# Scan stage: sample gate and old states in column tiles, new states in 32-row tiles, decay on GpSimd, clip per head

## The chip, the cores and the metric

The kernel runs on one core of one Trainium2 chip. The metric is device time in microseconds (us), the median of the runs. Five engines run side by side and wait for each other through semaphores: TensorE (PE; its weight loads are listed as PEld), VectorE (DVE), ScalarE (ACT), GpSimd (POOL) and SyncE (SP), which here only issues DMAs.

## What is computed

One step of a hybrid decoder layer for a prompt of 512 tokens and eight sample sequences of eight tokens: a combined input projection, latent attention, a Mamba-2 scan (SSD), a mixture of experts and two norms, all in float32. The change is in the scan. From the reference, cut:

```python
a_cs = jnp.cumsum(dt * a, axis=2)
seg = a_cs[:, :, :, None] - a_cs[:, :, None, :]
decay_ls = jnp.exp(jnp.where(causal[:, :, None, None], seg, -jnp.inf))
cb = jnp.einsum('bclgn,bcsgn->bclsg', cm, bm)
w_ls = cb[..., None] * decay_ls * dt[:, :, None]
y_diag = jnp.einsum('bclsgh,bcsghp->bclghp', w_ls, x)
states = jnp.einsum('bclgn,bclgh,bclghp->bcghpn', bm, decay_end * dt, x)
...
    return d_c[..., None, None] * h + s_c, h
...
y_off = jnp.einsum('bclgn,bcghpn->bclghp', cm, h_prev) * jnp.exp(a_cs)[..., None]
...
y = y.reshape(b, t, D_INNER) * jax.nn.silu(z.astype(jnp.float32))
y = rms_norm(y.reshape(b, t, SSD_GROUPS, D_INNER // SSD_GROUPS), ...)
```

There are four groups of eight heads (`G`, `HG`), a head has 64 channels (`PD`), a state 128 entries (`NST`). The prompt goes in four chunks of 128 tokens. A sample sequence is one chunk of eight tokens with an old state from `state_ssm`, and its new state is an output.

## The kernel before

The program is a chain of stages, each with one instruction stream per engine and a barrier of all engines behind it. `stage_ssd` holds the scan. It runs over N = 20 units k = (g, i): four groups g of five tiles i, the tiles 0 to 3 being prompt chunks of 128 tokens (called P0 to P3 in the prediction) and tile 4 the 64 sample tokens (called S). In a group the prompt tiles pass a state `stT` along; tile 4 works with the old states `h0` of the eight sequences (four blocks of 128 channels, eight sequences, 128 entries).

The order on every engine is that of the code, written as a software pipeline over k. TensorE does per iteration: `inputs(k)` (four transposes of x into bank 0, L1426; B turned and C·B in bank 1, L1432 and L1433; for tile 4 the decays at the sequences' ends, L1439), `gate(k-1)` (eight products with the weights `wz` into bank 7, L1452), `turn(k-2)` (four transposes of the normed y, L1521) and `outputs(k-1)` (eight heads, L1464, into bank 4; state times C, L1467, into bank 5; the chunk's own state, L1470, into bank 6). A float32 product shows as two records in the trace.

For tile 4 `outputs` goes on: the final prompt state is turned (L1475) and copied by ScalarE to `st_out` (L1585); then for each of the eight sequences four transposes of its old state (L1489, alternately into banks 7 and 6), a copy to `h0T` on ScalarE (L1591) and a product with `c_of` (L1498), where C is masked to the sequence's tokens, summed in bank 5 of all 64 rows. Then eight products of `xend` and `b_of` (B masked by sequence, 64 rows), L1507, alternately into banks 6 and 7, each followed by an addition to `h0` on VectorE (L1703). The gate of the next group's tile 0 stands behind all eight (`hs_out`).

VectorE does per iteration k: copies of B and C·B (L1652, L1653), the clip of the decay exponents `dec` (subtract, L1663; minimum with 0, L1665), then, when ScalarE has taken the exponential (L1559), the product with C·B (L1668). Then for unit k-1: for tile 4 the aging of the old states, `h0` times `e_seq` (L1677), the output (from L1679 to the gate's product, L1690), the states (L1694, L1696, or L1703 for tile 4) and the norm (L1708, L1710, L1713). ScalarE: copy of x (L1557), exponential of `dec` (L1559), SiLU of the gate (L1567), copy of the turned y to `yT` (L1574, shown as xbcT), the copies above, square and root (L1595, L1597). The three functions each load a table. GpSimd scales x in three ways (L1390) and masks C and B (L1395, L1398). SP issues the decays of unit k+3 once unit k's output is ready, for tile 4 then the stores of `st_out` and, behind `hs_out`, of `h0`, and behind their landing the loads of the next group's old states.

## Time and profile before

| | us |
|---|---|
| median of 3 runs (2594.32 to 2598.78) | 2597.01 |
| the profiled execution's own time | 2604.68 |
| its span, first to last instruction | 2602.9 |
| its mean granted TensorE clock (share of 2.4 GHz) | 0.946 |
| TensorE busy in the span | 2404.9 (92%) |
| VectorE busy | 1838.8 (71%) |
| ScalarE busy | 1325.8 (51%) |
| GpSimd busy | 463.4 (18%) |

The scan stage lies between about 724 and 1117 us of the span. The time at which an engine is busy over the whole span says little about it; it has to be read from its own stretch. In a timeline a row gives the start, the length, the engine with the line and operation, what is written and read, and in brackets how long the engine was idle before and what released it. Rows of several instructions are merged (x16). Durations of matmuls overlap, since they are pipelined; the distance between starts is what one costs. In the rows by stretch the columns are: stretch, us, then busy time (and count) of PE, PEld, DVE, ACT and POOL, the granted clock, the share of the DMA engines, GB/s.

### The profile page before, as it was taken

Reading aid. Unit: us, or ns where it says so; the run is one execution under the profiler, and the core shown is the slowest. Engines: PE = TensorE matmul, PEld = TensorE weight load, DVE = VectorE, ACT = ScalarE, POOL = GpSimd, SP = SyncE. Lnnn points to the kernel's source line nnn. Section 1 sums busy time; section 2 is a strip of 40 time slices with the busy share of each in tenths; the row PEclk is TensorE's granted clock in tenths of the full one; section 3 lists DMA queues with packets and bytes.
Section 4 is the critical chain, followed back from the end, with each engine's and each line's share of the span. In section 5 each row is a group of like instructions: output and inputs, shape, how many; then the busy total and the mean of one; then the engine's idle time right before and its main releaser. Section 6 shows DMA issues by size and latency. Waiting matters only on the chain. (4 is left out here: it accounts for less than half of the span.)

```text
span 2602.9 us, 38413 instructions
## 1 busy us (share of the span) xinstructions
PE 2404.9 (92%) x14463; PEld 1889.6 (73%) x14463; DVE 1838.8 (71%) x2099; ACT 1325.8 (51%) x1410; POOL 463.4 (18%) x372
## 2 busy tenths in 40 slices
PE   8798999989969999979898999999999999999993
...
DMA packets 248575, 589.80 MB, mean 227 GB/s; under 512 B 28880, under 2 KB 120272, under 8 KB 243984
## 3 DMA queue, kind: packets, MB, share of 16 engines
...
## 5 line engine op out<-in xcount | busy, mean ns | idle before, releaser
L2418 DVE TENSOR_TENSOR w_lo<-w_raw,w_hi 128x2048 fp32r<-128x2048 f32 x291 | 660.2, 2289 | 56.1 <-ACT w_hi L2368 54.5
L2368 ACT ACTIVATE w_hi<-w_raw 128x2048 fp32r<-128x2048 f32 x288 | 550.2, 1916 | 130.4 <-PE banks L2311 118.7
L2311 PE MATMUL banks<-w_hi,x_hi 128*128 128x512 f32 x1024 | 319.9, 394 | 2.1 <-DVEq L2457 2.1
L2311 PE MATMUL banks<-w_lo,x_hi 128*128 128x512 f32 x1024 | 316.9, 391 | 0.0
L2311 PE MATMUL banks<-w_hi,x_lo 128*128 128x512 f32 x1024 | 316.3, 390 | 0.0
L2418 DVE TENSOR_TENSOR w_lo<-mergedT,w_hi 128x2048 fp32r<-128x2048 f32 x96 | 220.0, 2292 | 40.0 <-ACT w_hi L2368 39.8
L2311 PEld LDWEIGHTS banks<-w_hi,x_lo 128*128 128x128 f32 x1024 | 192.8, 188 | 41.0
L2311 PEld LDWEIGHTS banks<-w_lo,x_hi 128*128 128x128 f32 x1024 | 192.8, 188 | 40.9
L2311 PEld LDWEIGHTS banks<-w_hi,x_hi 128*128 128x128 f32 x1024 | 190.5, 189 | 40.0 <-DVEq L2457 2.1
L2271 POOL DMA_INDIRECT y_sum<-xT,to_row x32 | 50.9, 1590 | 845.6 <-ACT xT L2400 845.6
L2368 ACT ACTIVATE w_hi<-mergedT 128x2048 fp32r<-128x2048 f32 x96 | 183.8, 1915 | 34.0 <-PE banks L2311 30.5
L2311 PE MATMUL banks<-w_hi,h_hi 128*128 128x512 f32 x512 | 158.5, 391 | 0.0
L2311 PE MATMUL banks<-w_hi,h_lo 128*128 128x512 f32 x512 | 158.0, 390 | 0.0
L2311 PE MATMUL banks<-w_lo,h_hi 128*128 128x512 f32 x512 | 157.7, 389 | 0.0
L1452 PE MATMUL banks<-wz,xT 128*128 128x512 f32 (+1 forms) x320 | 147.8, 616 | 0.9 <-ACT zs L1567 0.9
L1452 PEld LDWEIGHTS banks<-wz,xT 128*128 128x128 f32 (+1 forms) x320 | 58.6, 188 | 76.3 <-issue 75.9
L2311 PEld LDWEIGHTS banks<-w_lo,h_hi 128*128 128x128 f32 x512 | 96.1, 188 | 20.8
L2311 PEld LDWEIGHTS banks<-w_hi,h_hi 128*128 128x128 f32 x512 | 96.0, 188 | 20.8 <-DVE w_lo L2418 0.3
L2311 PEld LDWEIGHTS banks<-w_hi,h_lo 128*128 128x128 f32 x512 | 96.1, 188 | 20.0
L1390 POOL TENSOR_TENSOR xdt<-xs_t,dt 128x512 f32<-128x512 f32 (+1 forms) x20 | 26.1, 1304 | 427.2 <-ACT xs_t L1557 427.2
L1034 PE MATMUL banks_a<-part_hi_a,w_mhi_a 128*128 128x288 f32 x384 | 83.2, 298 | 14.5 <-DVE w_mlo_a L1070 14.5
L1070 DVE TENSOR_TENSOR w_mlo_a<-w_raw_a,w_mhi_a 128x1024 fp32r<-128x1024 f32 x24 | 29.4, 1225 | 85.0 <-ACT w_mhi_a L1044 85.0
...
## 6 DMA issues: line engine op xcount, KB each, us to landing
...
```

Source lines behind the costliest of these rows:

```text
L1034: mm = pe.matmul(bank_of(u)[:, piece], wp[:, u % NW, k, :], part[:, piece * H2:(piece + 1) * H2], start=(k == 0 and wp is w_hi and n == 0) ...
L1070: dve.tensor_tensor(w_lo[:, u % NW], w_raw[:, u % NR], w_hi[:, u % NW].bitcast(F32), ALU.subtract).then_inc(w_low, 1)
L1390: ins = pool.tensor_tensor(heads(o[0:n, k % 2], n), x, f[:, g * HG:(g + 1) * HG].unsqueeze(2).broadcast_to((n, HG, PD)), ALU.mult)
L1452: mm = pe.matmul(banks[0:n, 7, :], sb.xT[:, q, P * i:P * i + n], wz[:, g % 2, q, :], start=(q == 0), stop=(q == KD - 1))
L2271: pool.indirect_dma_start(out=io.y_sum, out_offset=bass.IndirectOffsetOnAxis(ap=to_row[:, par, :].bitcast(U32), axis=0), in_=y_out, in_off ...
L2311: mm = pe.matmul(banks[:, bank + c, :], x[:, k, :], part[:, s % NHI, j, c * 512:(c + 1) * 512], start=start, stop=last)
L2368: act.activation(w_hi[:, s % NHI], raw(s, par), ACT.Copy).then_inc(hi_ready, 1)
L2418: dve.tensor_tensor(w_lo[:, s % NHI], raw(s, par), w_hi[:, s % NHI].bitcast(F32), ALU.subtract).then_inc(lo_ready, 1)
```

## The change

For the sample tile (i = 4):

- The gate is computed in two column tiles: 256 output columns each, with the 64 tokens on PSUM partitions 0 to 63 and 64 to 127 of bank 7, sixteen products of 256 columns for eight of 512. SiLU takes the two halves apart.
- Old states are turned in pairs j and j + 4 (eight transposes), into banks 2 and 3 or 6 and 7, copied to `h0T` (four places for two) by ScalarE and VectorE, one each, and multiplied with 32 columns of `c_of`, into partitions 0 to 31 and 32 to 63 of bank 5.
- New states: eight products of 32 rows in pairs (`new_part`, q = 0 to 3), the first pair at the end of `outputs`, the second behind the next `inputs`, the last two behind the next `gate`. The additions to `h0` go into `renew`, the first four ahead of the unit's norm, the last four behind it. The wait of the next gate for them is gone; a wait for the first six stands in `outputs` of the next group's tile 0.
- `h0` times `e_seq` goes to GpSimd, behind `b_of` and ahead of the next unit's scaling.

For every tile the clip is one instruction per head that subtracts the head's own sum and takes the minimum with 0, eight instructions for two. `c_of`, `e_seq` lie in the room of `t1` to `t3`, and a constant of four columns is added.

```diff
+        NEW_BANK = (2, 5, 5, 2)
...
-                        pool.tensor_tensor(c_of[:], sb.xbcT[:, 20 + g, SEQ:T].unsqueeze(1).broadcast_to((P, NSEQ, NS)),
-                                           K[:, K_BCOL:K_BCOL + NSEQ * NS].rearrange("p (b n) -> p b n", b=NSEQ), ALU.mult)
+                            pool.wait_ge(st_ready, NT * g)
+                        pool.tensor_tensor(c_of.rearrange("p (a b) x -> p a b x", a=2),
+                                           sb.xbcT[:, 20 + g, SEQ:T].rearrange("p (a x) -> p a x", a=2).unsqueeze(2).broadcast_to((P, 2, 4, 32)),
+                                           K[:, K_BCOL:K_BCOL + NSEQ * NS].rearrange("p (b n) -> p b n", b=NSEQ)[:, 0:4, 0:32].unsqueeze(1).broadcast_to((P, 2, 4, 32)),
+                                           ALU.mult)
                         pool.wait_ge(cb_out, k + 1)
-                        pool.tensor_tensor(b_of[:], b_t[0:NS, k % 2, :].unsqueeze(1).broadcast_to((NS, NSEQ, NST)),
-                                           K[0:NS, K_BROW:K_BROW + NSEQ].unsqueeze(2).broadcast_to((NS, NSEQ, NST)), ALU.mult).then_inc(of_seq, 1)
+                        pool.tensor_tensor(b_of[:], b_t[0:NS, k % 2, :].unsqueeze(1).broadcast_to((NS, 4, NST)),
+                                           K[0:NS, K_BMOD:K_BMOD + 4].unsqueeze(2).broadcast_to((NS, 4, NST)), ALU.mult).then_inc(of_seq, 1)
+                        pool.wait_ge(e_out, g + 1)
+                        for j in range(4):
+                            pool.wait_ge(hT_ready, 4 * g + j + 1)
+                            for b in (j, j + 4):
+                                ins = pool.tensor_tensor(h0[:, :, b, :], h0[:, :, b, :], e_seq[:, :, b:b + 1].broadcast_to((P, 4, NST)), ALU.mult)
+                            ins.then_inc(aged, 1)
...
-                    if g >= 1 and i == 0:
-                        pe.wait_ge(hs_out, 8 * g)
+                    if i == NT - 1:
+                        for q in range(KD):
+                            for c in range(2):
+                                mm = pe.matmul(banks[64 * c:64 * (c + 1), 7, 0:GW // 2], sb.xT[:, q, SEQ:T], wz[:, g % 2, q, c * (GW // 2):(c + 1) * (GW // 2)],
+                                               start=(q == 0), stop=(q == KD - 1))
+                        mm.then_inc(z_ready, 1)
+                        return
...
+                        if g >= 1 and i == 0:
+                            pe.wait_ge(hs_out, 8 * g - 2)
                         pe.matmul(banks[0:n, 5, :], sb.xbcT[:, 20 + g, at], stT[:], start=True, stop=True).then_inc(y_ready, 1)
-                        if g >= 1 and i == 0:
-                            pe.wait_ge(hs_out, 8 * g)
...
-                    def turn_state(b):
-
-                        if b == 0:
+                    def turn_states(j):
+
+                        if j == 0 and g >= 1:
+                            pe.wait_ge(hs_out, 8 * g)
+                        elif j == 1:
+                            pe.wait_ge(fin_out, g + 1)
                             pe.wait_ge(z_out, k + 1)
-                        elif b == 1:
-                            pe.wait_ge(fin_out, g + 1)
-                        else:
-                            pe.wait_ge(hT_out, NSEQ * g + b - 1)
-                        for q in range(4):
-                            mm = pe.transpose(banks[:, 7 - b % 2, q * P:(q + 1) * P], h0[:, q, b, :], K[:, K_ID:K_ID + P])
+                        elif j >= 2:
+                            pe.wait_ge(hT_out, 4 * g + j - 1)
+                            pe.wait_ge(hT_out2, 4 * g + j - 1)
+                        for a, b in enumerate((j, j + 4)):
+                            for q in range(4):
+                                mm = pe.transpose(banks[:, (2, 6)[j % 2] + a, q * P:(q + 1) * P], h0[:, q, b, :], K[:, K_ID:K_ID + P])
                         mm.then_inc(hT_ready, 1)
 
-                    turn_state(0)
-                    for b in range(NSEQ):
-                        m = NSEQ * g + b
-                        if b + 1 < NSEQ:
-                            turn_state(b + 1)
-                        pe.wait_ge(hT_out, m + 1)
-                        mm = pe.matmul(banks[0:n, 5, :], c_of[:, b, :], h0T[:, b % 2, :], start=(b == 0), stop=(b == NSEQ - 1))
-                        mm.then_inc(off_part, 1)
-                        if b == NSEQ - 1:
-                            pe.wait_ge(off_part, m + 1)
-                            pe.sem_inc(y_ready, 1)
-                    for u in range(8):
-                        q, half = divmod(u, 2)
-                        if u >= 2:
-                            pe.wait_ge(hs_out, 8 * g + u - 1)
-                        mm = pe.matmul(banks[:, 6 + u % 2, :], xend[0:n, k % 2, q * P:(q + 1) * P], b_of[:, 4 * half:4 * half + 4, :],
+                    def old_part(j):
+                        pe.wait_ge(hT_out, 4 * g + j + 1)
+                        pe.wait_ge(hT_out2, 4 * g + j + 1)
+                        for a, b in enumerate((j, j + 4)):
+                            mm = pe.matmul(banks[32 * a:32 * (a + 1), 5, :], c_of[:, b, :], h0T[:, 2 * (j % 2) + a, :], start=(j == 0), stop=(j == 3))
+                        mm.then_inc(off_part if j < 3 else y_ready, 1)
+
+                    turn_states(0)
+                    turn_states(1)
+                    old_part(0)
+                    old_part(1)
+                    turn_states(2)
+                    turn_states(3)
+                    old_part(2)
+                    old_part(3)
+                    new_part(k, 0)
+
+                def new_part(k, q):
+
+                    g = unit(k)[0]
+                    if q == 1:
+                        pe.wait_ge(y_step, 2 * k + 1)
+                    elif q >= 2:
+                        pe.wait_ge(hs_out, 8 * g + (0, 0, 4, 2)[q])
+                    for a in range(2):
+                        mm = pe.matmul(banks[:, NEW_BANK[q] + a, :], xend[32 * a:32 * (a + 1), k % 2, q * P:(q + 1) * P], b_of[32 * a:32 * (a + 1)],
                                        start=True, stop=True)
-                        mm.then_inc(hs_ready, 1)
-                    pe.wait_ge(hs_ready, 8 * g + 8)
-                    pe.sem_inc(st_ready, 1)
+                    mm.then_inc(hs_ready if q < 3 else st_ready, 1)
...
+                    late = k >= 2 and unit(k - 2)[1] == NT - 1
                     if k < N:
                         inputs(k)
+                    if late:
+                        new_part(k - 2, 1)
                     if 1 <= k <= N:
                         gate(k - 1)
+                    if late:
+                        new_part(k - 2, 2)
+                        new_part(k - 2, 3)
...
+                            for m in range(4):
+                                act.wait_ge(hT_ready, 4 * g + m + 1)
                                 if m >= 2:
-                                    act.wait_ge(off_part, m - 1)
-                                act.activation(h0T[:, b % 2, :], banks[:, 7 - b % 2, :], ACT.Copy).then_inc(hT_out, 1)
+                                    act.wait_ge(off_part, 3 * g + m - 1)
+                                elif g >= 1:
+                                    act.wait_ge(y_ready, NT * g)
+                                act.activation(h0T[:, 2 * (m % 2), :], banks[:, (2, 6)[m % 2], :], ACT.Copy).then_inc(hT_out, 1)
...
+                def renew(j, q):
+                    g = unit(j)[0]
+                    if q < 3:
+                        dve.wait_ge(hs_ready, 3 * g + q + 1)
+                    else:
+                        dve.wait_ge(st_ready, j + 1)
+                    for a in range(2):
+                        old = h0[:, q, 4 * a:4 * a + 4, :].rearrange("p b n -> p (b n)")
+                        dve.tensor_tensor(old, old, banks[:, NEW_BANK[q] + a, :], ALU.add).then_inc(hs_out, 1)
...
-                        own = acs[0:n, i, g * HG:(g + 1) * HG].unsqueeze(2).broadcast_to((n, HG, n))
                         dve.wait_ge(dec_in[k % 3], 16 * (k // 3 + 1))
-                        dve.tensor_tensor(seg, seg, own, ALU.subtract).then_inc(seg_step, 1)
-                        dve.wait_ge(seg_step, k + 1)
-                        dve.tensor_scalar(seg, seg, 0.0, None, ALU.min).then_inc(seg_out, 1)
+                        for h in range(HG):
+                            own = acs[0:n, i, g * HG + h:g * HG + h + 1]
+                            ins = dve.tensor_scalar(seg[:, h, :], seg[:, h, :], own, 0.0, ALU.subtract, ALU.min)
+                        ins.then_inc(seg_out, 1)
...
-                                dve.wait_ge(hT_ready, NSEQ * g + b + 1)
-                                dve.tensor_tensor(h0[:, :, b, :], h0[:, :, b, :], e_seq[:, :, b:b + 1].broadcast_to((P, 4, NST)), ALU.mult).then_inc(aged, 1)
+                            for m in range(4):
+                                dve.wait_ge(hT_ready, 4 * g + m + 1)
+                                if m >= 2:
+                                    dve.wait_ge(off_part, 3 * g + m - 1)
+                                elif g >= 1:
+                                    dve.wait_ge(y_ready, NT * g)
+                                dve.tensor_copy(h0T[:, 2 * (m % 2) + 1, :], banks[:, (3, 7)[m % 2], :]).then_inc(hT_out2, 1)
...
-                            for u in range(8):
-                                q, half = divmod(u, 2)
-                                dve.wait_ge(hs_ready, 8 * g + u + 1)
-                                old = h0[:, q, 4 * half:4 * half + 4, :].rearrange("p b n -> p (b n)")
-                                dve.wait_ge(aged, NSEQ * (g + 1))
-                                ins = dve.tensor_tensor(old, old, banks[:, 6 + u % 2, :], ALU.add)
-                                ins.then_inc(hs_out, 1)
                             if g + 1 < G:
                                 dve.memset(stT[:], 0.0).then_inc(st_new, 1)
+                            dve.wait_ge(aged, 4 * (g + 1))
+                            renew(j, 0)
+                            renew(j, 1)
...
+                        if i == NT - 1:
+                            renew(j, 2)
+                            renew(j, 3)
```

How the order moves. TensorE from the gate of a sample tile to its second output of an old state, before:

```order
L1452 MATMUL banks<-wz,xT 64x512 x8
L1521 MATMUL banks<-const,y 128x128 x4
L1464 MATMUL banks<-xdt,dec 64x64 x8
L1475 MATMUL banks<-const,stT 128x128 x4
L1489 MATMUL banks<-const,h 128x128 x8
L1498 MATMUL banks<-h0T,c_of 64x512
L1489 MATMUL banks<-const,h 128x128 x4
L1498 MATMUL banks<-h0T,c_of 64x512
```

and of the changed kernel:

```order
L1464 MATMUL banks<-wz,xT 64x256 x16
L1549 MATMUL banks<-const,y 128x128 x4
L1481 MATMUL banks<-xdt,dec 64x64 x8
L1492 MATMUL banks<-const,stT 128x128 x4
L1509 MATMUL banks<-const,h 128x128 x16
L1516 MATMUL banks<-h0T,t 32x512 x4
L1509 MATMUL banks<-const,h 128x128 x16
L1516 MATMUL banks<-h0T,t 32x512 x4
```

The gate is 16 records of 64x256 in place of 8 of 64x512, and the transposes and outputs of old states come in blocks of two pairs each (here 16 transposes, then 4 outputs) in place of one after another.

TensorE from the last outputs of old states to the turn behind the next group's first gate, before:

```order
L1498 MATMUL banks<-h0T,c_of 64x512 x2
L1507 MATMUL banks<-b_of,xend 128x512 x8
L1426 MATMUL banks<-const,xbcT 128x128 x4
L1432 MATMUL banks<-const,xbcT 128x128
L1433 MATMUL banks<-xbcT 128x128
L1452 MATMUL banks<-wz,xT 128x512 x8
L1521 MATMUL banks<-const,y 128x64 x4
```

and of the changed kernel:

```order
L1516 MATMUL banks<-h0T,t 32x512 x4
L1537 MATMUL banks<-b_of,xend 128x512 x2
L1438 MATMUL banks<-const,xbcT 128x128 x4
L1444 MATMUL banks<-const,xbcT 128x128
L1445 MATMUL banks<-xbcT 128x128
L1537 MATMUL banks<-b_of,xend 128x512 x2
L1469 MATMUL banks<-wz,xT 128x512 x8
L1537 MATMUL banks<-b_of,xend 128x512 x4
L1549 MATMUL banks<-const,y 128x64 x4
```

The eight products of new states (`b_of`, `xend`) stood ahead of `inputs` and gate; now two stand ahead, two between `inputs` and gate, four behind the gate.

VectorE over a sample tile, from the last clip instruction or the product behind it (`dec`), before:

```order
L1665 TENSOR_SCALAR dec<-dec 128x1024
L1668 TENSOR_TENSOR dec<-dec,cb 128x1024
L1677 TENSOR_TENSOR h<-h,e_seq 128x4x128 x8
L1679 TENSOR_TENSOR off<-banks,e_acs 64x512
L1685 TENSOR_TENSOR y<-off,xd 64x512
L1687 TENSOR_TENSOR y<-y,banks 64x512
L1690 TENSOR_TENSOR y<-y,zs 64x512
L1703 TENSOR_TENSOR h<-h,banks 128x512 x8
L1706 MEMSET stT 128x512
L1708 TENSOR_SCALAR ssq<-ssq 64x1
L1710 RECIPROCAL ssq<-ssq 64x1
L1713 SCALAR_TENSOR_TENSOR y<-y,ssq,gn 64x512
```

and of the changed kernel:

```order
L1719 TENSOR_TENSOR dec<-dec,cb 128x1024
L1732 COPY h0T<-banks 128x512 x4
L1734 TENSOR_TENSOR off<-banks,e_acs 64x512
L1740 TENSOR_TENSOR y<-off,xd 64x512
L1742 TENSOR_TENSOR y<-y,banks 64x512
L1745 TENSOR_TENSOR y<-y,zs 64x512
L1754 MEMSET stT 128x512
L1692 TENSOR_TENSOR h<-h,banks 128x512 x4
L1759 TENSOR_SCALAR ssq<-ssq 64x1
L1761 RECIPROCAL ssq<-ssq 64x1
L1764 SCALAR_TENSOR_TENSOR y<-y,ssq,gn 64x512
L1692 TENSOR_TENSOR h<-h,banks 128x512 x4
```

The eight agings have left for GpSimd with four copies `h0T` in their place, and the additions to `h` stand four ahead and four behind the norm.

## Rows read from the trace of the kernel before

**Rows 1.** Busy time by engine in one group (L1452 start to start); columns as told above.
```profile
928.81:1020.95 92.14, 87.32 (x316) 42.81 (x316) 57.95 (x87) 41.53 (x60) 26.48 (x17) 0.89 0.32 99
```

**Rows 2.** Timeline of prompt tiles in the second group: start, length, engine, line, [wait <-releaser].
```profile
862.28 0.63 PE L1426 MATMUL banks<-const,xbcT 128*128 128x128 f32 x4 [0.78 <-ACT xbcT L1574]
...
867.34 1.67 DVE L1663 TENSOR_TENSOR dec<-dec,acs 128x1024 f32<-128x1024 f32 x1
...
867.89 2.02 POOL L1390 TENSOR_TENSOR xend<-xs_t,w_end 128x512 f32<-128x512 f32 x1
...
869.04 1.42 DVE L1665 TENSOR_SCALAR dec<-dec 128x1024 f32<-128x1024 f32 x1
...
870.49 1.06 ACT L1559 ACTIVATE dec<-dec 128x1024 f32<-128x1024 f32 x1 [2.66 <-DVE dec L1665]
...
873.23 0.69 DVE L1679 TENSOR_TENSOR off<-banks,e_acs 128x512 f32<-128x512 f32 x1 [0.43 <-PE banks L1467]
```

**Rows 3.** Timeline from P3 over the sample tile to P0' of the third group.
```profile
885.80 0.69 DVE L1679 TENSOR_TENSOR off<-banks,e_acs 128x512 f32<-128x512 f32 x1 [1.15 <-PE banks L1467]
...
887.32 7.08 PE L1452 MATMUL banks<-wz,xT 128*64 128x512 f32 x16
...
892.04 0.28 DVE L1653 TENSOR_TENSOR cb<-banks,const 128x128 f32<-128x128 f32 x1
...
892.24 1.66 DVE L1663 TENSOR_TENSOR dec<-dec,acs 128x1024 f32<-128x1024 f32 x1
...
898.49 0.71 PE L1489 MATMUL banks<-const,h 128*128 128x128 f32 x4 [1.84 <-ACT zs L1567]
898.73 0.58 ACT L1585 ACTIVATE st_out<-banks 128x512 f32<-128x512 f32 x1
...
904.49 1.07 PE L1498 MATMUL banks<-h0T,c_of 128*64 128x512 f32 x2
...
912.90 0.68 DVE L1679 TENSOR_TENSOR off<-banks,e_acs 64x512 f32<-64x512 f32 x1 [1.26 <-PEq L1502]
...
927.03 0.69 DVE L1703 TENSOR_TENSOR h<-h,banks 128x512 f32<-128x512 f32 x1 [1.02 <-PE banks L1507]
...
928.81 9.14 PE L1452 MATMUL banks<-wz,xT 128*128 128x512 f32 x16
...
934.04 1.23 DVE L1668 TENSOR_TENSOR dec<-dec,cb 128x1024 f32<-128x1024 f32 x1 [1.12 <-ACT dec L1559]
...
941.22 0.69 DVE L1679 TENSOR_TENSOR off<-banks,e_acs 128x512 f32<-128x512 f32 x1 [5.95 <-PE banks L1467]
```

**Rows 4.** Timeline of TensorE in the sample attention stage, two forms of array tiles.
```profile
316.56 0.66 PE L683 MATMUL banks<-keyT,q 32*64 32x256 f32 x8 [1.41 <-issue]
317.15 0.43 PE L695 MATMUL banks<-rows,mergedT 128*64 128x256 f32 x1
...
317.42 0.38 PE L695 MATMUL banks<-rows,mergedT 128*64 128x256 f32 x1
317.43 0.38 PE L695 MATMUL banks<-rows_ahead,mergedT 128*64 128x256 f32 x1
317.63 0.38 PE L695 MATMUL banks<-rows,mergedT 128*64 128x256 f32 x1
```

**Rows 5.** Groups of instructions by form: 32-column tiles ahead of the scan (busy us, mean ns).
```profile
L1412 PE MATMUL banks<-const,dta 128*32 128x128 f32 x8 | 0.7, 420 | 0.0
```

**Rows 6.** Timeline of VectorE in the routing stage: per-partition operands, 128 columns.
```profile
1373.85 1.37 DVE L2033 TENSOR_SCALAR w_raw<-const,mergedT 128x128 f32<-128x128 f32 x5
```

**Rows 7.** Timeline of GpSimd at the scan's start, with VectorE idle or on short operations.
```profile
743.45 1.04 POOL L1390 TENSOR_TENSOR xdt<-xs_t,dt 128x512 f32<-128x512 f32 x1 [202.75 <-ACT xs_t L1557]
```

**Rows 8.** Busy time by engine, PEclk as eighth column, from the sample's off on.
```profile
912.90:927.80 14.90, 13.06 (x19) 4.83 (x20) 8.08 (x13) 2.01 (x3) 0.00 (x0) 0.60 0.21 53
```

**Rows 9.** Timeline of SP at the end of the scan stage.
```profile
1107.53 3.94 SPq L1343 DMA_DIRECT2D out<-h  x4
...
1117.52 17.54 SPq L1016 DMA_DIRECT2D w_raw_a<-in_w_in  x5
```

33 lines of the change are left out of this document (18 added, 15 removed).

## The prediction

> **Names.** A group is five units of work, the prompt tiles P0 to P3 and the sample tile S; P0' to P3' belong to the group behind. "Off" is the start of VectorE's first operation on a unit's output (L1679), the mark by which I measure. Stamps are those of the second group unless said; the third repeats it.
>
> **What bounds the kernel now.** Stages are separated by barriers, and all edits are in the scan stage, so I read only that stage: first the busy time by stretch, then the timeline of one prompt unit, then that of one sample unit with what ended each wait. The third group takes 92.1 us from gate to gate [rows 1], and so does the second. 27.1 of them pass from P3's off to S's (885.80 to 912.90) and 28.3 from S's to that of P0' (912.90 to 941.22) [rows 3], which leaves 36.7 us for the three steps between prompt tiles, 12.2 each (the last one is 12.57, 873.23 to 885.80) [rows 2, 3]. In a prompt unit two chains are nearly equal. TensorE's own work (inputs from 862.28, gate, turn, outputs, next inputs possible about 11.6 us later) is one. The other goes from VectorE's off through clip (L1663, L1665), ScalarE's exponential, which waits 2.66 us for the clip, SiLU and the yT copy to TensorE's next inputs, whose row ends a wait on that copy [rows 2]. The second chain spans two units, so a microsecond in it is worth half a one per unit, and at most what TensorE waits (0.78 us at 862.28). In the sample unit everything waits in turn: TensorE 1.84 us for SiLU, then eight sequences one after another to S's off, then eight additions on VectorE, and only then the gate of P0' (928.81), with VectorE idle 5.95 us before the off of P0' [rows 3]. That is where the change works.
>
> **Do tiles of the array run side by side?** The same form as the new sample gate, 128 rows by 64 columns with 256 moving columns, starts in pairs 0.01 us apart (317.42, 317.43), the next pair 0.21 behind [rows 4]: 32 records are 16 pairs, 3.5 us, against 7.08 in [rows 3]. Four 32-column tiles run together too (eight records of L1412 busy for 0.7 us, 0.42 us each) [rows 5], and so do 32-row tiles: eight records of 32x64 with 256 columns take 0.66 us, where in turn they would take eight times 0.21 [rows 4]. So I price a pair of 32-column tiles (old states' output) or of 32-row tiles (new states) as one matmul: two records of 0.43, 0.86 us. No row shows 32x128 alone; its bounds are 0.86 a pair and 1.72 if the two go in turn.
> Does a change of tile form cost? The last eight 32x64 records start at 316.56 and the first 128x64 one at 317.15 [rows 4]; the eight need about 0.45 us of array, so at most some 0.1 us is lost. For some eight such changes in a group I charge 0.7 us. The Trainium skill (TensorEngine Tiling (Array Packing), Key Properties) says that changing the tiling mode, unlike the tile, drains TensorE, which speaks against mixing modes as this change does; by that rule the drain is real, by the rows it is no longer than this, and with none at all the sum would be 2 us better.
>
> **Part by part, from P3's off (885.80).**
> 1. *To S's off.* VectorE reaches the clip of P0' at 892.24, unchanged. Subtract and minimum took 3.12 us, to 895.36. Now there are eight instructions of 128x128 with a pointer operand. Five such stand in 1.37 us (0.257 each, with two pointers) [rows 6]; a plain 128-column one starts 0.20 behind its forerunner (892.04 to 892.24) [rows 3]. I take 0.23: 1.9 us, done at 894.2. GpSimd, beside whose scaling L1663 and L1665 take longer (rival A), now waits for the first turned states at that time, so it holds none of these. From the clip's end to the end of the st_out copy took 3.95 us (895.36 to 899.31); the second half of SiLU adds 0.1: 898.25. TensorE is earlier: gate S, begun at 887.32, ends at 890.8, but its turn waits for P3's norm, which ends just ahead of cb (892.04); heads, final state and the first pair of turned states (banks 2 and 3, no wait on SiLU) end near 895. It then waits for st_out, until 898.25. Behind that: a pair of turns (8 transposes at 0.113, 0.9), two outputs (1.72), two pairs of turns (1.8), two outputs (1.72): 904.4. The copies h0T go half to VectorE, half to ScalarE, 0.6 to 0.7 us each, under the next turns. S's off at 904.4 instead of 912.90: 8.5 us won. The aging left VectorE, where it had lain in waits (eight of 0.69 us): nothing won or lost by it there.
> 2. *To the last state addition.* Was 912.90 to 927.72, 14.8 us. Now TensorE goes new 0 (0.86), inputs (0.8), new 1 (0.86), gate P0' (6.9), new 2 (0.86): 914.7. VectorE meanwhile does four output operations (2.9), memset (0.5), additions 0 and 1 (four of 0.72), norm (1.4), to 912.0, waits, then does the last four additions (2.9) to 917.6: 13.2 us, 1.6 won. What is queued behind this wait is the clip of P1', and behind that ScalarE's exponential, SiLU of P0' and the yT copy of S.
> 3. *To the off of P0'.* Was 13.5 us, with the gate inside and 5.95 us of idleness. Now the gate is done, and VectorE needs b_t and cb (0.4), clip (1.9), exponential (1.1), product (1.25): 922.3, against 941.22. In all 18.9 us won. The step to P1' stays: TensorE waits for the yT copy of S until 923.1 and reaches the next off 10.8 us later, 933.9, 11.6 us behind the last.
> 4. *GpSimd.* A 128x512 product alone takes 1.04 us (743.45) and up to 2.02 beside VectorE [rows 2, 7]. Aging is eight such: two behind each pair of turns. The first two cannot start before the product of P0' is done (about 896.3), the last two follow the fourth turn; done at 905.6 to 906. VectorE wants them at 907.8: hidden by 2 us. The scaling of P0' moves behind it (to 909), TensorE wants it at 916.
> 5. *SP.* The stores of h wait for the last addition and hold the loads of the next old states and the next decays: those come 10 us earlier than before and are wanted 17 us earlier. The decays of P3' are wanted by its clip alone, two units behind P1', and the old states four units behind: hidden.
> 6. *Prompt units.* Clips are 1.2 us shorter if GpSimd doesn't step between (0.5 us per unit won, 1 to 1.5 per group), 1.0 longer if it does (rival A). I take nothing.
> 7. *Clock.* TensorE idles 3 us ahead of the second pair and 3.5 us ahead of P1's gate. Before, it ran at 1.2 GHz through much of 912.9 to 927.8 (granted 0.60) [rows 8], which stretched the gate behind to 9.14 us [rows 3]. I charge 1.7 us of doubled work more than before.
>
> Per group 18.9 - 0.7 - 1.7 = 16.5 us, three times: 49.5. The last group has no gate behind: S's off 7.5 us earlier; then ten instead of 14.5 us to the stores (1107.53), which the next stage waits for (1117.52) [rows 9]: 12, less 1 for clock and switches, 11. **Sum 60.5 us.** The profiled execution took 2604.68 (span 2602.9), so about 2544; it lies 7.7 us above the median of the runs, 2597.01, from which I forecast **2536**.
>
> **Rivals.**
> A. *GpSimd steps between the eight clips.* For: xend took 2.02 us where L1663 and then L1665 stood beside it, and those took 1.67 and 1.42 [rows 2]: they take turns. Eight short instructions give it eight openings; it has two operations left (0.94 each), so the clip ends 1.0 us later than now. Half of it per prompt unit and all of it for P1' comes to 11 us: 2547. Against: nothing is to be waited for between the clips. The Trainium skill (SBUF — State Buffer, section on the two separate sides) calls the pair of ports that the two share an exclusive lock for a whole instruction; the trace agrees with whole instructions, and who wins between short ones no row shows.
> B. *Aging becomes the bound.* At 2.02 us each, eight end at 912.5 and the additions wait 4.7 us: four groups, 19 us, 2555. Against: VectorE's operations at that time read PSUM, save three.
> C. *Tiles go in turn.* Old outputs +3.4, new states +2.6 on the path, 6 us a group: 2560. [rows 4, 5] speak against it. That is also the case in which the change doesn't do what it says.
> D. *Slower, by the clock.* Shorter matmul phases between waits of 3 us keep TensorE at 1.2 GHz. From 16.5 us of TensorE work per group on that run at half the clock more than now, all is lost; with four gates (27.5 us) at half, each of three groups loses 11 and the last about 5: 2635. Against: the full clock held from 903 to the new states through turns and outputs with waits between.
>
> **How the numbers follow.** Forecast 0.75, A 0.11, B 0.07, C 0.04, D 0.03. Best ends (no charge for clock and switches, clips short) give 76 us; half clock for 10 us a group and A together leave 39. So 2520 to 2558, which also holds A and B. A measurement tells about 0.2% from no change: faster 0.95, within it 0.02, slower 0.03, the last two from D.
>
> **What would show it.** Offs of the same tile about 75.6 us apart from group to group; 32 gate records in 3.5 us with starts in pairs; S's off some 18.6 us behind P3's, and P0's some 18 behind that; no wait of VectorE on aging; eight clips in 2 us and GpSimd's xend still near 1 to 2 us; the next stage's first load near 1057. It is wrong if pairs start 0.4 us apart, if L1509 or the gates of P0 and P1 show doubled durations for long, or if the additions wait for GpSimd.

## The result, and the profile after

The changed kernel takes **2556.43 us** (median of four runs, 2551.27 to 2564.04) against 2597.90 for the kernel before (four runs, 2594.32 to 2604.14): ratio 0.984, 95% interval 0.9807 to 0.9874. That is 41.5 us faster. The forecast was 2536, 61 us faster; the measured time lies near the upper end of its range.

The profiled execution took 2559.46 us (span 2557.7). I measure the scan stage from the start of its first load (dt_b) to that of the next stage's first load (w_raw_a). Timeline of SP in the kernel after, at both ends and at the last stores of h:

```profile
722.84 0.37 SPq L1325 DMA_DIRECT2D dt_b<-in_ssd_dt_bias  x1
...
1058.63 3.95 SPq L1347 DMA_DIRECT2D out<-h  x4
...
1068.61 0.38 SPq L1018 DMA_DIRECT2D w_raw_a<-in_w_in  x1
```

That is 345.8 us. The same rows before were at 723.61 and 1117.52 [rows 9], 393.9 us. So the stage gave **48.1 us** where the sum said 60.5, and 2.9 us went elsewhere: what lies behind the stage took 1485.4 us before and 1489.1 after, and it varies from 1484.6 to 1489.3 among all the profiles of this study, so I don't explain it.

Busy time by engine in one group of after (start of the gate of P0' to the next such; columns start:end, length, TensorE, its weight loads, VectorE, ScalarE, GpSimd, PEclk, DMA share, GB/s), to be laid beside [rows 1]:

```profile
898.20:976.75 78.55, 69.61 (x334) 38.75 (x332) 55.33 (x113) 39.41 (x56) 27.59 (x26) 0.96 0.38 117
```

92.14 us became 78.55. TensorE's busy time fell by 17.7, from 87.32 to 69.61: the column tiles of the gate and of the old states' output, the row tiles of the new states, and less of the lower clock (mean 0.96 instead of 0.89). Its waits grew from 4.8 to 8.9 us.

The next fence is the timeline of the second group of after from P3's off over the sample tile to the inputs of P2' (start, length, engine, line, tiles, and in brackets the wait and its releaser), to be laid beside [rows 3]:

```profile
874.41 0.69 DVE L1734 TENSOR_TENSOR off<-banks,e_acs 128x512 f32<-128x512 f32 x1 [0.47 <-PE banks L1486]
...
876.67 3.67 PE L1464 MATMUL banks<-wz,xT 128*64 128x256 f32 x32
...
880.85 1.65 DVE L1715 TENSOR_SCALAR dec<-dec,acs 128x128 f32<-128x128 f32 x8
...
886.83 1.50 PE L1509 MATMUL banks<-const,h 128*128 128x128 f32 x8 [3.06 <-ACT st_out L1624]
...
888.27 3.13 PE L1516 MATMUL banks<-h0T,t 128*32 128x512 f32 x8
...
891.33 1.97 PE L1509 MATMUL banks<-const,h 128*128 128x128 f32 x16
...
893.31 1.93 PE L1516 MATMUL banks<-h0T,t 128*32 128x512 f32 x8
...
895.27 0.68 DVE L1734 TENSOR_TENSOR off<-banks,e_acs 64x512 f32<-64x512 f32 x1 [1.24 <-PE banks L1516]
...
898.20 7.13 PE L1469 MATMUL banks<-wz,xT 128*128 128x512 f32 x16
...
899.05 2.41 DVE L1692 TENSOR_TENSOR h<-h,banks 128x512 f32<-128x512 f32 x4
...
906.44 2.48 DVE L1692 TENSOR_TENSOR h<-h,banks 128x512 f32<-128x512 f32 x4 [3.72 <-PE banks L1537]
...
909.24 2.46 DVE L1715 TENSOR_SCALAR dec<-dec,acs 128x128 f32<-128x128 f32 x8
...
913.96 0.68 DVE L1734 TENSOR_TENSOR off<-banks,e_acs 128x512 f32<-128x512 f32 x1
...
915.12 1.09 PE L1438 MATMUL banks<-const,xbcT 128*128 128x128 f32 x4 [3.77 <-ACT xbcT L1613]
...
916.64 7.75 PE L1469 MATMUL banks<-wz,xT 128*128 128x512 f32 x16
```

The gate in column tiles took 3.67 us for its 32 records, beside 7.08 for 16 records of twice the columns: the two column tiles did run side by side. From P3's off to S's off 20.86 us instead of 27.10; from there to the off of P0' 18.69 instead of 28.32. In the place of the long chain of states stand three waits: TensorE's 3.06 us for the st_out copy, VectorE's 3.72 for the second half of the new states, and TensorE's 3.77 for the yT copy.

All five steps of the second group, from one off to the next (us):

| step | before | after |
|---|---|---|
| P0 to P1 | 11.81 | 13.57 |
| P1 to P2 | 12.32 | 12.35 |
| P2 to P3 | 12.57 | 13.08 |
| P3 to S | 27.10 | 20.86 |
| S to P0' | 28.32 | 18.69 |
| sum | 92.1 | 78.55 |

So the sample tile and what follows it gave 15.9 us, and the prompt tiles took 2.3 back. The third group repeats this within 0.03 us a step. The first group gave less, 92.7 to 79.6 us, since its step P3 to S was only 25.74 us long before. In the last group, which has no gate behind it, the step P3 to S went from 22.95 to 16.06 us, and from S's off to the end of the stage it took 24.49 before and 21.09 after.

### The profile page after: what moved, and what is told of

Its sections match the earlier page's. It is cut to its first block and busy times, and to the rows that moved or that the text cites. A ratio compares the mean times of both kernels' runs of the same rounds, so it can differ in the third digit from the quotient of the medians.

```text
span 2557.7 us, 38662 instructions
## 1 busy us (share of the span) xinstructions
PE 2340.9 (92%) x14527; PEld 1875.0 (73%) x14527; DVE 1830.9 (72%) x2203; ACT 1317.5 (52%) x1398; POOL 467.3 (18%) x404
## 3 DMA queue, kind: packets, MB, share of 16 engines
q8 instruction: 84, 1.38, 0.2%
## 5 line engine op out<-in xcount | busy, mean ns | idle before, releaser
L1469 PE MATMUL banks<-wz,xT 128*128 128x512 f32 x256 | 115.5, 604 | 1.3 <-ACT zs L1606 1.3
L2365 PEld LDWEIGHTS banks<-w_hi,h_hi 128*128 128x128 f32 x512 | 96.5, 189 | 21.9 <-issue 0.7
L1469 PEld LDWEIGHTS banks<-wz,xT 128*128 128x128 f32 x256 | 48.6, 195 | 58.7 <-issue 58.6
## 6 DMA issues: line engine op xcount, KB each, us to landing
wz<-in_w_in SPq DMA_DIRECT2D x4, 2048.0 KB, 11.7
```

The source lines that it names most:

```text
L1469: mm = pe.matmul(banks[0:n, 7, :], sb.xT[:, q, P * i:P * i + n], wz[:, g % 2, q, :], start=(q == 0), stop=(q == KD - 1))
L2365: mm = pe.matmul(banks[:, bank + c, :], x[:, k, :], part[:, s % NHI, j, c * 512:(c + 1) * 512], start=start, stop=last)
```

## The experiments

All have the same measure beside the time: the length of the scan stage as defined above, and the steps from off to off in the second group. The single times are of the profiled run.

| kernel | time, us | scan stage | P0-P1 | P1-P2 | P2-P3 | P3-S | S-P0' |
|---|---|---|---|---|---|---|---|
| before | 2604.68 | 393.9 | 11.81 | 12.32 | 12.57 | 27.10 | 28.32 |
| after | 2559.46 | 345.8 | 13.57 | 12.35 | 13.08 | 20.86 | 18.69 |
| after, clip in two | 2556.63 | 344.6 | 13.78 | 11.81 | 13.08 | 21.21 | 18.96 |
| after, scaling late | 2544.38 | 335.5 | 13.61 | 11.58 | 12.38 | 19.44 | 17.87 |
| after, whole gate | 2553.28 | 343.9 | 12.34 | 12.34 | 13.08 | 19.15 | 18.69 |
| after, aging on VectorE | 2563.24 | 357.5 | 13.80 | 12.35 | 13.08 | 23.77 | 18.69 |
| after, new states first | 2567.22 | 354.1 | 12.35 | 12.34 | 13.08 | 22.1 | 21.9 |
| before, clip per head | 2612.42 | 398.5 | 12.35 | 12.34 | 14.10 | 27.77 | 26.72 |
| before, tiled gate | 2601.85 | 391.4 | 11.82 | 12.32 | 12.58 | 28.13 | 26.85 |
| before, scaling late | 2601.46 | 386.7 | 11.58 | 11.58 | 12.38 | 27.8 | 26.79 |

The kernel before took on the same chips: 2594.47 (clip in two, scaling late, whole gate, new states first) and 2601.61 (aging, and the three made from before). From the third row on each kernel ran once. The other groups need not repeat the second: a step with a stretch of TensorE at the lower clock changes by 1 to 2 us between groups of one run (P2-P3 is 13.08 us in two groups of the run with the whole gate and 14.78 in the other two). So a difference of 1 or 2 us in the stage shows little by itself, and I go by the steps and rows.

### Who steps between the eight clips

The theory was rival A: GpSimd's scaling of a unit (xdt, xend, xd) gets its operation in after each short instruction of VectorE and holds the next one until it is done. The first rival to it: the eight short instructions themselves cost the time. Two kernels tell them apart. One takes back the clip's form:

```diff
-for h in range(HG):
-    own = acs[0:n, i, g * HG + h:g * HG + h + 1]
-    ins = dve.tensor_scalar(seg[:, h, :], seg[:, h, :], own, 0.0, ALU.subtract, ALU.min)
-ins.then_inc(seg_out, 1)
+dve.tensor_tensor(seg, seg, own, ALU.subtract).then_inc(seg_step, 1)
+dve.wait_ge(seg_step, k + 1)
+dve.tensor_scalar(seg, seg, 0.0, None, ALU.min).then_inc(seg_out, 1)
```

> The changed kernel with the clip of before (subtract, then minimum, two instructions over all heads). Measure: scan stage from SP's first load (dt_b) to the next stage's first load (w_raw_a), 393.9 us before, 345.8 changed. Theory A (GpSimd's scaling steps between the eight clips): prompt clips 3.65 -> 3.1 us, the sample's 4.55 -> 3.1, that of P0' 1.65 -> 1.95; half of the prompt gain counts, so some 1.2 us per group less, stage about 341. Rival (the missing microseconds are the half clock and waits of TensorE; the clip's form is no matter): stage within 1 us of 345.8.

It came to 344.6 us, nearer to the rival than to theory A. The clips were 3.12 us for P2 and P3, 2.06 for S, 1.94 for P0' and 2.74 for P1', where the kernel after has 3.65, 4.55, 1.65 and 2.46. For the prompt tiles P2 and P3 and for S they are shorter, for P0' and P1' longer. The step P1-P2 shrank by 0.53 us, and P3-S and S-P0' grew by some 0.3 each, so that in all the form of the clip is worth 1.2 us of the stage, not the 5 that I expected. The other kernel keeps the eight instructions and takes GpSimd away from them:

```diff
 pool.wait_ge(xs_out, k + 1)
+pool.wait_ge(seg_out, k + 1)
```

> The changed kernel with one wait more: GpSimd's scaling of unit k waits for the clip of unit k. Theory A: every clip 1.65 us, steps between prompt tiles down to TensorE's own 11.6 to 12.2 us, the sample's off to that of P0' 0.8 less; GpSimd may now stand beside the product and the output operations; stage 336 to 341. Rival (half clock and TensorE's waits hold the missing time): within 1 us of 345.8.

335.5 us, 10.3 less, just below the range of theory A. First P2' of the third group in the kernel after, timeline of GpSimd, VectorE and ScalarE:

```profile
919.66 1.32 POOL L1394 TENSOR_TENSOR xdt<-xs_t,dt 128x512 f32<-128x512 f32 x1 [9.21 <-ACT xs_t L1591]
...
920.39 3.65 DVE L1715 TENSOR_SCALAR dec<-dec,acs 128x128 f32<-128x128 f32 x8
...
920.94 1.04 POOL L1394 TENSOR_TENSOR xend<-xs_t,w_end 128x512 f32<-128x512 f32 x1
...
921.94 1.04 POOL L1394 TENSOR_TENSOR xd<-xs_t,d_b 128x512 f32<-128x512 f32 x1
...
924.08 1.06 ACT L1593 ACTIVATE dec<-dec 128x1024 f32<-128x1024 f32 x1 [3.20 <-DVE dec L1715]
```

And the same tile in the run with the scaling late:

```profile
911.02 1.65 DVE L1716 TENSOR_SCALAR dec<-dec,acs 128x128 f32<-128x128 f32 x8
...
912.70 1.06 ACT L1594 ACTIVATE dec<-dec 128x1024 f32<-128x1024 f32 x1 [1.20 <-DVE dec L1716]
...
912.80 1.04 POOL L1395 TENSOR_TENSOR xdt<-xs_t,dt 128x512 f32<-128x512 f32 x1 [5.91 <-DVE dec L1716]
...
913.79 1.23 DVE L1720 TENSOR_TENSOR dec<-dec,cb 128x1024 f32<-128x1024 f32 x1 [1.12 <-ACT dec L1594]
...
913.80 2.12 POOL L1395 TENSOR_TENSOR xend<-xs_t,w_end 128x512 f32<-128x512 f32 x1
```

With GpSimd at work the eight instructions take 3.65 us, with GpSimd held back 1.65. GpSimd is busy until 922.98, 2.59 us into the clip; in that time VectorE gets three of the eight through, and the other five follow in the last 1.0 us, 0.2 each. ScalarE's wait for the clip is longer by just the difference, 3.20 against 1.20. The clip of S, which has more operations of GpSimd beside it, fell from 4.55 to 1.38 us. The scaling now falls on the product dec·cb, where xend gives way (2.12 us) and VectorE doesn't (1.23).
This also says where the 10.3 us are. VectorE clips a unit ahead of the off of the unit before it, so the clip of P1' stands in the step S-P0', which shrank by 0.82, and that of P3 in P1-P2, which shrank by 0.77. P2-P3 shrank by 0.70, but not by S's own clip, which ends in time even at 4.55 us: in the kernel after TensorE's inputs of S come 1.37 us behind P2's off, since they wait for a yT copy that is queued behind P3's exponential, and 0.66 us behind it with the scaling late. The two rows, the first from the kernel after and the second from this run:

```profile
862.70 0.60 PE L1438 MATMUL banks<-const,xbcT 128*64 128x128 f32 x4 [1.31 <-ACT xbcT L1613]
...
855.43 0.60 PE L1439 MATMUL banks<-const,xbcT 128*64 128x128 f32 x4
```

Together that is 2.3 us a group, and with the second clip of the stage 8.4 in all. The rest of the gain lies in stretches of TensorE at the lower clock, below: the step P3-S is 1.42 us shorter in two of the first three groups, and in the last group it is 1.71 longer (17.77 for 16.06), with the turned states there at the lower clock.

The clip's form and GpSimd's time apart, in the kernel before:

```diff
-dve.tensor_tensor(seg, seg, own, ALU.subtract).then_inc(seg_step, 1)
-dve.wait_ge(seg_step, k + 1)
-dve.tensor_scalar(seg, seg, 0.0, None, ALU.min).then_inc(seg_out, 1)
+for h in range(HG):
+    own = acs[0:n, i, g * HG + h:g * HG + h + 1]
+    ins = dve.tensor_scalar(seg[:, h, :], seg[:, h, :], own, 0.0, ALU.subtract, ALU.min)
+ins.then_inc(seg_out, 1)
```

> The kernel before, with one edit of the change alone: the clip as eight instructions of one head in place of two of eight heads. Scan stage 393.9 us before. Theory 1 (GpSimd's scaling wins after every short instruction and holds the next one for its whole 1.04 us): clips of 3.65 us in prompt units and 3.65 to 4.6 for P0', against 3.12, so 1 to 3 us more per group, 397 to 405. Rival (fewer elements read and written, so a shorter clip, as the sum took it): 1.2 us less in the clip of P0' and half of it per prompt unit, about 3 us less per group, 380 to 386.

398.5 us: 4.6 us **slower** than before. P2-P3, the step in which S is clipped, is 1.5 us longer in each of the four groups (14.10 for 12.57). The part of the change that looks safest, fewer elements through VectorE, is a loss by itself. The row of S's clip in this run, with the operations of GpSimd that came between (eight short instructions of 64x64 that should need less than 1.4 us):

```profile
879.80 6.11 DVE L1664 TENSOR_SCALAR dec<-dec,acs 64x64 f32<-64x64 f32 x8
...
880.10 1.03 POOL L1390 TENSOR_TENSOR xend<-xs_t,w_end 64x512 f32<-64x512 f32 x1
...
881.10 1.03 POOL L1390 TENSOR_TENSOR xd<-xs_t,d_b 64x512 f32<-64x512 f32 x1
...
882.10 1.26 POOL L1395 TENSOR_TENSOR c_of<-xbcT,const 128x512 f32<-128x512 f32 x1
...
883.33 1.89 POOL L1398 TENSOR_TENSOR b_of<-b_t,const 64x1024 f32<-64x1024 f32 x1
```

GpSimd goes from one operation to the next without a gap (880.10 to 885.2), and VectorE gets one short instruction in between two of them. And the wait of GpSimd alone, in the kernel before:

```diff
 pool.wait_ge(xs_out, k + 1)
+pool.wait_ge(seg_out, k + 1)
```

> The kernel before, with GpSimd's scaling of a unit made to wait until VectorE has clipped that unit's decays. Theory 1 (GpSimd in the clip costs time in the kernel before too): clips of 2.1 instead of 3.12 us, 1 us won in that of P0' and half of it per prompt unit, 1.5 to 2.5 us per group, scan stage 384 to 388 against 393.9. Rival (the scaling then comes too late for the heads' outputs, or the exponential is what the chain waits for): 394 or more.

386.7 us, 7.2 less than before, with clips of 1.94 instead of 3.12 us. So the contention was there in the kernel before too, and one line takes it away. So most of the 10.3 us that this line gives in the kernel after are no loss that the change brought: some 7 were to be had before it as well. The whole time of this run (2601.46, beside 2601.61 for the kernel before) does not show it: what lies ahead of the stage took 726.1 us in it and 723.6 in the profile of before, what lies behind it 1486.9 and 1485.4. With one run each I claim only the stage.

### What the sample gate in column tiles is worth

In the kernel after, the sample gate made whole again, with its SiLU in one piece (the short diff stands for both):

```diff
-if i == NT - 1:
-    for q in range(KD):
-        for c in range(2):
-            mm = pe.matmul(banks[64 * c:64 * (c + 1), 7, 0:GW // 2], sb.xT[:, q, SEQ:T], wz[:, g % 2, q, c * (GW // 2):(c + 1) * (GW // 2)],
-                           start=(q == 0), stop=(q == KD - 1))
-    mm.then_inc(z_ready, 1)
-    return
```

> The changed kernel with the sample gate and SiLU as before (eight products of 512 columns). Theory (from the sum's first step: TensorE waits 3.06 us for st_out behind the shorter gate, so its 3.5 us are hidden): stage 345.8 to 348. Rival (the shorter gate is on the path): 3.5 us per group, stage about 360.

343.9 us, below both expectations: 1.9 us less with a gate that takes 3.4 us longer. In the first three groups nothing of the gate's saving reaches S's off, because S's chain runs through clip, exponential, SiLU and st_out copy, and TensorE merely waits for it; their steps P3-S are 1.7 to 1.9 us shorter with the whole gate. In the last group no clip of a next unit stands in the chain, and there the gate is on the path: the turn of P3's output, which follows it, starts 1.6 us later with the whole gate, and the step P3-S is 17.65 us for 16.06. The rows of gate and turn in the last group, first after (P3's off at 1031.46), then with the whole gate (P3's off at 1025.79):

```profile
1032.32 3.67 PE L1464 MATMUL banks<-wz,xT 128*64 128x256 f32 x32
1037.63 0.66 PE L1549 MATMUL banks<-const,y 128*128 128x128 f32 x4 [1.64 <-DVE y L1764]
...
1026.54 7.08 PE L1462 MATMUL banks<-wz,xT 128*64 128x512 f32 x16
1033.56 0.66 PE L1542 MATMUL banks<-const,y 128*128 128x128 f32 x4
```

In the three other groups the wait has a price. TensorE in the run with the whole gate does the first eight outputs of old states in 2.0 us and less; in the kernel after the same eight took 3.13 us (the row at 888.27 above), close behind its wait of 3.06 us, and the granted clock says why. First the kernel after, from the end of that wait to the end of those outputs, and the inputs and gate behind the other long wait of TensorE; columns as in the windows above:

```profile
886.83:891.33 4.50, 4.50 (x16) 1.64 (x16) 0.69 (x1) 1.04 (x2) 2.06 (x2) 0.62 0.00 0
915.12:924.23 9.11, 9.11 (x24) 4.81 (x25) 7.87 (x18) 4.13 (x7) 3.33 (x3) 0.84 0.85 231
```

A clock of 0.62 is a stretch spent mostly at 1.2 GHz. In the final version below, where only 0.92 us of wait stand ahead, the same 16 records and the start of a 17th have:

```profile
876.75:879.70 2.95, 2.95 (x17) 1.18 (x17) 0.69 (x1) 1.02 (x2) 2.95 (x4) 1.00 0.01 3
```

4.50 against 2.95: 1.55 us per group. In the inputs and gate of P1' the lower clock costs 1.2 to 1.5 us more: in the run with the whole gate the step P0-P1 was 12.34 in the group where that gate took 7.03 us and 13.8 in the two where it took 8.73, and in the kernel after, with a gate of 7.75, it is 13.57.
What these runs show of it: in the kernel after, with the clip in two and with the new states first, all nine groups with a gate behind (3.06 or 3.35 us of wait for st_out) had these outputs at 3.11 to 3.63 us. With the whole gate none had. But of the three groups with the scaling late, which have the same wait of 3.06 us, one did part of this work at the lower clock and two at the full one. A wait of 3 us is therefore not enough for it; something else decides too, and I did not find out what. No run has the whole gate and a long wait together, so whether the form of the gate itself plays a part stays open.

The same gate in column tiles, done alone in the kernel before:

> The kernel before, with the sample gate in two column tiles (3.5 us in place of 7.1) and its SiLU in two halves, all else as it was. Theory 1 (the sample gate lies beside the chain of VectorE and ScalarE that ends in st_out, so nothing hangs on it but TensorE's clock): scan stage 392 to 396 us against 393.9, and possibly one to two us a group more where the shorter gate brings a half-clock stretch. Rival (the gate's 3.5 us are on the path): 380 to 383.

391.4 us, 2.5 less, and just below the range of theory 1. The step P3-S became 1.0 us longer (28.13) and S-P0' 1.5 shorter (26.85), so the gate's 3.4 us are again not in the sum of these groups; what moved are the stretches at the lower clock, of which I did not pursue each. In the last group P3-S is 1.6 us shorter (21.35 for 22.95), as in the kernel after.

### Does the order of the new states matter

In the kernel after, TensorE does all four pairs of new states ahead of the gate of P0', and VectorE all additions ahead of its norm:

```diff
 if late:
     new_part(k - 2, 1)
+    new_part(k - 2, 2)
+    new_part(k - 2, 3)
 if 1 <= k <= N:
     gate(k - 1)
-if late:
-    new_part(k - 2, 2)
-    new_part(k - 2, 3)
```

> The changed kernel with all four pairs of new states ahead of the next gate and all eight additions ahead of the norm. Theory 1 (moving half of them behind the gate hides them): the gate starts 5 us later and the sample's off to that of P0' grows by 4 to 5 us in three groups, stage about 360. Theory 2 (VectorE only waits 3.72 us behind the norm for the late pairs, and that wait is what the early order removes; TensorE had room): that step stays or falls by 1 us and the next one by 1 to 2, stage 340 to 346.

354.1 us, between the two expectations, 8.3 more than the kernel after. Not all of it is the edit's: 3.7 of the 8.3 stand in the steps P3-S, which the edit doesn't touch and where this run was longer at the lower clock. Putting two of the pairs behind the gate is worth the rest, some 5 us. Timeline of TensorE in this run, second group:

```profile
905.82 3.40 PE L1537 MATMUL banks<-b_of,xend 32*128 32x512 f32 x8 [3.23 <-DVE h L1691]
909.15 9.06 PE L1469 MATMUL banks<-wz,xT 128*128 128x512 f32 x16
```

TensorE waits 3.23 us for banks that VectorE's additions have to free, and then does pairs and gate at the lower clock: 3.40 instead of 1.99 us and 9.06 instead of 7.13. The wait of 3.23 us costs 3.3 us more in clock. In return P0-P1 is 12.35 for 13.57.

### What moving the aging to GpSimd is worth

In this kernel VectorE ages two old states behind its copy of each pair of turned states, and the loop on GpSimd is gone:

```diff
+for b in (m, m + 4):
+    ins = dve.tensor_tensor(h0[:, :, b, :], h0[:, :, b, :], e_seq[:, :, b:b + 1].broadcast_to((P, 4, NST)), ALU.mult)
+ins.then_inc(aged, 1)
```

> The kernel after, with the aging of the old states back on VectorE: behind each pair of its copies of turned states it ages the two states itself, and GpSimd has none of it. Scan stage (first load of dt_b to first load of the next stage) 345.8 us in the kernel after. Theory 1 (the aging's move pays twice: it keeps VectorE's copies and S's off free of 1.4 us per pair, and it holds GpSimd's scaling away from the clip of P0'): the clip of P0' goes from 1.65 to about 4.5 us and some three pairs of agings lie in the chain to S's off, so 3 to 6 us more per group, 358 to 370. Rival, the prediction's own words (the aging had lain in waits, nothing won or lost by its move): 345 to 347.

357.5 us, 11.7 more, just below the range of theory 1. Timeline of TensorE and VectorE in this run:

```profile
879.30 3.65 DVE L1709 TENSOR_SCALAR dec<-dec,acs 128x128 f32<-128x128 f32 x8
...
887.29 1.94 PE L1503 MATMUL banks<-const,h 128*128 128x128 f32 x8 [5.06 <-ACT st_out L1618]
...
895.55 1.05 PE L1510 MATMUL banks<-h0T,t 128*32 128x512 f32 x4 [0.75 <-DVE h0T L1726]
```

Of the 2.9 us that the step P3-S grew, 0.75 is TensorE's wait for a copy that stands behind an aging. The greater part is the clip of P0': 3.65 instead of 1.65 us, so TensorE waits 5.06 for st_out instead of 3.06. In the kernel after, GpSimd waits for turned states at the time of that clip, as the prediction says. So in the first three groups the aging on GpSimd gains more by keeping GpSimd from the clip at the right time than by relieving VectorE. In the last group, which has no clip there, the relief alone shows: the step P3-S is 17.88 us with the aging on VectorE and 16.06 without. The four steps P3-S together make 11.2 of the 11.7 us.

### Putting it together

Three versions follow from this, each timed against the kernel before on one chip. With the scaling late and the gate whole:

> The kernel after with two edits: GpSimd's scaling waits for the clip, as in the run with that edit alone (scan stage 335.5 us, step to S's off 19.44 and once 20.76 us), and the sample gate is whole again, 7.1 us in place of 3.7. Theory 1 (the gate of S lies beside the chain through clip, exponential, SiLU and st_out copy; a shorter one only makes TensorE wait 3.06 us, behind which it ran at the lower clock in some groups): the wait is gone, the step to S's off 18.2 to 19.5 us, scan stage 331 to 336. Rival (with the clip short the gate is on the path, and its 3.5 us show): 20.5 to 22.5 us per step, scan stage 341 to 346.

Ratio to the kernel before 0.977, 95% 0.9745 to 0.9794; scan stage 331.6 us, steps P3-S 19.11 in all three groups. Theory 1 holds: with the wait down to 0.51 us no group did the first outputs at the lower clock.

The next one follows from the wait of 3.72 us that VectorE has in the kernel after ahead of its last four additions. The clip of P1' is queued behind them and needs nothing of what is waited for, so it goes into that wait.

```diff
 if i == NT - 1:
+    if k + 1 < N:
+        clip(k + 1)
     renew(j, 2)
     renew(j, 3)
```

> The kernel after with two edits: GpSimd's scaling waits for the clip, and in each group VectorE does the clip of P1' ahead of the last four state additions, in the 3.7 us in which it waits for TensorE's second half of new states, not behind them. Against the run with the first edit alone (scan stage 335.5 us; steps to S's off 19.44, from there to the off of P0' 17.88, from there to that of P1' 13.7). Theory 1 (clip and exponential of P1' leave the path, and so do SiLU of P0' and the yT copy of S, which are queued behind that exponential on ScalarE and for which TensorE waits 3.77 us): step to P0' 15 to 16 us, step to P1' 11.5 to 13, 3 to 5 us per group, scan stage 320 to 327. Rival (TensorE, whose outputs of P0' and next inputs stand right behind, gives the time back in the step to P1'): group sum unchanged, 333 to 336.

Ratio 0.9746, 95% 0.9718 to 0.9774; scan stage 324.9 us. The step S-P0' is 15.29 instead of 17.87, and P0-P1 11.54 instead of 13.61: TensorE's wait for the yT copy is gone altogether. But P3-S rose to 21.19, with the sample gate still short: a wait of 3.06 us, and 3.58 us for the first outputs, as in the kernel after. (The chip of these last two kernels was slower ahead of the scan stage, 771 and 775 us to its start against 719 to 726 on the others; the kernel before took 2654.43 us on it.) That wait is what the whole gate takes away, so both together:

> The kernel after with three edits: GpSimd's scaling waits for the clip, the clip of P1' stands ahead of the last four state additions, and the sample gate is whole again. With the first two edits alone the scan stage took 324.9 us and the steps to S's off 22.08, 21.19, 21.00 us, in each of which TensorE waited 1.9 to 3.1 us for the st_out copy and then did the first eight outputs of old states in 3.5 to 3.6 us, as against 2.0 at the full clock. Theory 1 (the short gate leaves that wait, the wait is followed by the lower clock, and the gate itself is on no path): wait 0.6 us or less, the eight records in 2.0 us, steps of 19.0 to 19.5 us, scan stage 317 to 321. Rival (the lower clock there comes from somewhere else, or the gate's 3.5 us show): steps of 21 us or more, scan stage 324 or more.

**2534.5 us** (median of five, 2528.8 to 2540.59) against 2606.35 before on that chip, ratio 0.9728, 95% 0.9709 to 0.9746. Scan stage 320.3 us, steps of the second group 11.53, 11.58, 12.69, 19.52, 15.29, and 19.1 in the step P3-S of the first and third. The wait for st_out was 0.50 us in those two and 0.92 in the second group, a little over what theory 1 allows, and the eight records took 2.0 us in all three. The clip of P1' in it, and the additions behind, on VectorE:

```profile
891.00 1.64 DVE L1690 TENSOR_SCALAR dec<-dec,acs 128x128 f32<-128x128 f32 x8
...
894.80 2.48 DVE L1681 TENSOR_TENSOR h<-h,banks 128x512 f32<-128x512 f32 x4 [2.15 <-PE banks L1531]
```

Against the kernel before it is clearly ahead of the changed kernel (0.9728 to 0.984, though each on its own chip), and it keeps all of the change but the tiled gate. Three pairs of kernels now differ in the gate alone, and each time the whole gate has the shorter stage: 343.9 to 345.8, 331.6 to 335.5 and 320.3 to 324.9 us. With the tiled gate only in the last group, where the gate is on the path, some 1.5 us more should be won (an estimate from the steps 17.66 here and 16.20 in the run before); no run tried it.

## Why the prediction was right in kind and too large

The direction, the place (sample tile and what follows it) and most terms held. The stage gave 48.1 of 60.5 us, the median 41.5 of 61. The forecast overstates the gain by half; the measured time lies inside the range because the range is wide enough to hold rivals A and B as well. By the prediction's own steps:

1. *To S's off: 18.6 us by the sum, 20.86 measured.* Clip, exponential, SiLU and st_out copy held: TensorE went on 12.42 us behind P3's off, the sum has 12.45. Behind it the sum has 6.14 us of turns and outputs, the trace 8.44. 1.55 of that is the clock; the rest is a pair of outputs at 0.96 to 1.0 instead of 0.86 us and eight transposes at 1.0 instead of 0.9, which is where the changes of tile form are: with the full clock this stretch took 6.9 us in the final version, 0.7 above the sum, with three changes of form in it. I charged 0.7 for eight. By the Trainium skill (TensorEngine Tiling (Array Packing), Key Properties) a change of tiling mode drains TensorE: the trace allows that, at no more than 0.25 us for each.
2. *To the last addition: 13.2 by the sum, 13.65 measured.* TensorE's pairs, inputs and gate came 0.9 us later (pairs at 1.0 to 1.1, gate 7.13 instead of 6.9), the four additions took 2.48 instead of 2.9. The wait that I said would stand there does, 3.72 us, and the clip of P1' put into it was worth 4.7 us in the two steps behind (17.87 to 15.29 and 13.61 to 11.54). The prediction named what is queued behind the wait and then did not ask whether it has to be.
3. *To the off of P0': 17.9 by the sum, 18.69 measured, and 17.87 with GpSimd held back.* The difference is the clip of P1', 2.46 for 1.9. **"The step to P1' stays" failed.** P1's off was to be 10.8 us behind the yT copy; it was 12.4 behind it, since TensorE did inputs and part of the gate at the lower clock after its wait of 3.77 us. 11.81 became 13.57.
4. *GpSimd's aging hidden by 2 us: right.* Done 1.3 us behind S's off (896.59), wanted at 899.05. But "nothing won or lost by it there" was wrong: with the aging back on VectorE the stage is 11.7 us longer, about half of it (2.0 us in each of three groups) by way of the clip of P0'.
5. *SP hidden: right.* Behind the first unit, whose norm waits for a load (4.0 us at 765.11, 2.7 in the kernel before), no engine waits for a load in the stage.
6. *Prompt units, "I take nothing".* P1-P2 came out at 12.35 for 12.32, P2-P3 at 13.08 for 12.57. The mechanism is **rival A**, which had 0.11, and it does what its words say: after each short instruction GpSimd takes its turn, 1.04 us each, and a prompt clip is 3.65 us long for 3.12. I argued against it that "nothing is to be waited for between the clips", but it needs no wait: GpSimd's next operation stands ready and gets in before VectorE's next one. Its price of 11 us did not come: two long instructions in place of the eight give back 1.2 us of the stage in the kernel after (in the kernel before the eight cost 4.6). With GpSimd held back the stage gave 58.4 us, close to the 60.5 forecast, but that is luck: the same line gives 7.2 us in the kernel before, and the sum had none of it. The Trainium skill (SBUF — State Buffer, SBUF: two separate sides) says that the pair of ports goes for a whole instruction to the one that starts first; the trace agrees, and adds that between back-to-back short instructions of VectorE it was GpSimd that started first each time.
7. *Clock: charged 1.7 us per group, measured 1.55 at the turned states and some 1.2 at the gate of P1'.* The mechanism was right and the size 1 us per group too small. The prediction named the wait of 3 us behind the short gate, but took the gate's saving as free; it did not ask whether a gate as long as before would leave that wait away.

*Last group:* 11 by the sum, 8.0 measured. Step P3 to S gave 6.9 of 7.5, the tail behind S's off 3.4 of 4.5, and the prompt tiles took 2.3.

So where are the 12.4 us missing in the stage? In the second group the steps are longer than the sum has them by 2.3 us (P3-S), 0.8 (S-P0'), 1.8 (P0-P1) and 0.5 (P2-P3), less the 2.4 that were charged: 2.9 us, and about as much in the third and the last. The first group misses 3.4: its step P3-S was only 25.74 us long before, and the sum took its 8.5 us from the 27.10 of the second. Of the 5.4 us of a group 2.8 are lower clock, by the prices of point 7, 0.7 are the pairs and changes of form, 0.8 the clip of P1' beside GpSimd and 0.5 the step P2-P3, which shrinks when GpSimd is held back; the rest, 0.6 us, I can't place. Outside the stage 2.9 us are missing, and the two medians lie 3.8 us closer together than the two profiled runs; these I don't explain. Rivals B and C are out by points 4 and 1. Of D the mechanism is there at a tenth of the price.
